# A hybrid decoder step: the sample group's RWKV state update laid out as value half x token x head, with the group norm put between the last gate chunks

## What is computed

```python
def rwkv7_step(S, inp):                    # S: value x key, 64 x 64 for each token and head
    r_t, w_t, k_t, v_t, kk_t, a_t = inp
    sa = jnp.einsum('bhvk,bhk->bhv', S, -kk_t)
    S = (S * w_t[:, :, None, :] + sa[..., None] * (kk_t * a_t)[:, :, None, :]
         + v_t[..., None] * k_t[:, :, None, :])
    return S, jnp.einsum('bhvk,bhk->bhv', S, r_t)
...
mean = jnp.mean(o, axis=-1, keepdims=True)
var = jnp.mean(jnp.square(o - mean), axis=-1, keepdims=True)
o = ((o - mean) * lax.rsqrt(var + GN_EPS)).reshape(B, T, RW_WIDTH)
o = o * gn_w + gn_b
o = (o + bonus) * g
...
m = sigmoid(g_a) * (o_a @ w_pa) + sigmoid(g_b) * (o_b @ w_pb)
x = x + gt1 * (m @ w_o)
```

## Time and profile before

| | us |
|---|---|
| median of 3 runs | 1410.02 (1409.33 to 1414.19) |
| the profiled execution: its time | 1408.94 |
| its span | 1407.2 |
| TensorE busy | 1291.8 (92%) |
| VectorE busy | 461.1 (33%) |
| ScalarE busy | 316.7 (23%) |
| GpSimd busy | 71.5 (5%) |

### The profile page before, as it was taken

The page is one execution under the profiler, slowest core; times in us unless marked ns, Lnnn a source line. Parts: engine busy times, 40 slices in busy tenths (PEclk is TensorE's granted clock), DMA queues, the critical chain, the costliest instruction groups (busy, mean ns, idle before and its releaser), DMA issues.

```text
span 1407.2 us, 21314 instructions
## 1 busy us (share of the span) xinstructions
PE 1291.8 (92%) x8359; PEld 649.1 (46%) x8359; DVE 461.1 (33%) x1061; ACT 316.7 (23%) x563; POOL 71.5 (5%) x62
## 2 busy tenths in 40 slices
PE   6999768889797999999999999999999999999997
PEld 4887457867585333333333333333333333333333
DVE  2056533333635322332233222332223322233223
ACT  3014632200102221222122211222112221122212
POOL 0000701223200000000000000000000000000000
PEclk9999988999898999999999999999999999999999
DMA  9965130047513699999999999999999999999994
GB/s 368 318 232 212 38 120 2 3 153 271 213 60 120 246 416 429 428 428 428 428 428 428 428 428 428 428 428 428 429 428 429 428 429 428 429 428 429 428 428 173
DMA packets 55362, 465.44 MB, mean 331 GB/s; under 512 B 4989, under 2 KB 7297, under 8 KB 29706
## 3 DMA queue, kind: packets, MB, share of 16 engines
q1 hardware_dynamic: 53370, 461.09, 79.0%
q0 software_dynamic: 1408, 3.63, 0.8%
q10 hardware_dynamic: 544, 0.13, 0.0%
HBM read 462.36 MB, written 3.52 MB: 331 GB/s over the span
## 4 chain that ended last, share of the span: by engine, by line
PE 49%; DMA 42%; DVE 5%; ACT 2%; issue 1%; SPq 0%; POOL 0%; DVEq 0%; ACTq 0%
DMA ring<-in_w 40%; PE ps L1207 16%; PE ps L768 7%; PE ps L1233 5%; PE ps L1161 2%; PE ps L1119 2%; DMA ring<-in_w_mod 2%; PE ps L1098 2%; PE ps L1185 2%; PE ps L1072 1%; PE ps L777 1%; PE ps L745 1%; PE ps L1215 1%; PE ps L996 1%; DMA ring<-in_w_in 1%
## 5 line engine op out<-in xcount | busy, mean ns | idle before, releaser
L1207 PE MATMUL ps<-ring,PT 128*64 128x512 f32 x2048 | 449.8, 593 | 21.8 <-DMA ring<-in_w 21.0
L1207 PEld LDWEIGHTS ps<-ring,PT 128*64 128x64 f32 x2048 | 144.8, 137 | 320.8 <-issue 271.9
L1654 DVE TENSOR_TENSOR SQ<-ps,SQ 128x528 f32<-128x528 f32 x132 | 84.2, 700 | 626.4 <-PE ps L1185 626.4
L1233 PE MATMUL ps<-ring,PT 128*64 128x512 f32 x1024 | 226.8, 595 | 0.0
L1233 PEld LDWEIGHTS ps<-ring,PT 128*64 128x64 f32 x1024 | 70.5, 137 | 133.4 <-issue 133.4
L655 ACT COPY SG<-ps 128x512 f32<-128x512 f32 x64 | 34.4, 589 | 405.6 <-PE ps L1207 405.6
L768 PE MATMUL ps<-HT,ring 128*128 128x264 f32 x448 | 107.6, 401 | 1.9 <-DMA ring<-in_w_in 1.9
L768 PEld LDWEIGHTS ps<-HT,ring 128*128 128x128 f32 x448 | 87.8, 198 | 20.1 <-issue 2.6
L1161 PE MATMUL ps<-XR,PT 128*64 128x512 f32 x396 | 94.2, 611 | 1.6 <-DVE PT L1626 1.6
L1185 PE MATMUL ps<-PT 64*128 64x264 f32 x528 | 76.3, 408 | 0.8 <-ACT PT L668 0.8
L1185 PEld LDWEIGHTS ps<-PT 64*128 64x128 f32 x528 | 45.3, 185 | 44.9 <-issue 27.6
(11 more groups left out here) (375 smaller groups left out, 1130.5 us busy)
## 6 DMA issues: line engine op xcount, KB each, us to landing
ring<-in_w SPq DMA_DIRECT2D x192, 2048.0 KB, 20.9
ring<-in_w_mod SPq DMA_DIRECT2D x12, 2048.0 KB, 14.4
ring<-in_w_in SPq DMA_DIRECT2D x9, 2048.0 KB, 8.9
ring<-in_w_o SPq DMA_DIRECT2D x2, 2048.0 KB, 16.8
ring<-in_w_pa SPq DMA_DIRECT2D x1, 2048.0 KB, 7.8
ring<-in_w_pb SPq DMA_DIRECT2D x1, 2048.0 KB, 19.7
XR<-in_x_prompt SPq DMA_DIRECT2D x2, 512.0 KB
SG<-bias_by_distance POOLq DMA_DIRECT2D x1, 1024.0 KB, 9.0
```

The costliest lines, as they stand in the source:

```text
L1207: last = mm(ps[64 * lin:64 * lin + 64, 2 + hh, :], XG[:, k % 4, k // 4, :], slot_tile(c)[:, k % 2, lin * FE + hh * 512:lin * FE + hh * 512 ...
L1233: last = mm(ps[64 * hh:64 * hh + 64, 4, :], AC[:, f, :], slot_tile(c)[:, f % 4, hh * 512:hh * 512 + 512], start=(f == 0), stop=(f == NF - 1))
L1654: v.tensor_tensor(YA[:, p::4, :], ps[:, bank:bank + 2, 0:T], YA[:, p::4, :], ALU.add).then_inc(sem["comb_used"], 1)
```

## The change

The state now lies with (value half, token, head) on the 128 partitions and 32 values x 64 keys along the free axis. A vector over keys is then one row of 64 for each partition, and VectorE reads it with a stride of zero along the values (`over_values`), a vector over values with a stride of zero along the keys (`over_keys`). The rows come about once for all six vectors: GpSimd spreads each over (token, head) columns with 24 operations of 128x8x2 (L422 of the changed kernel, into `EXP`), TensorE turns them with 12 products of 64x64 into bank 4 (L959), and ScalarE copies that into `VEC` (three copies, L590 and L592), all ahead of the scan, next to `BON`. The five rounds of `EX` and `spread` fall away. Of the update, GpSimd computes two products (`SW`, `T2`, L450 and L451), VectorE the rest, from SBUF. The output goes back to (head parity, value) partitions with one operation of 128x128 (`SOE`) and one product of 128x32 on TensorE (L1100).

The state is loaded and stored with 2 transfers in place of 8, in rows of 8 KB in place of 256 bytes. The group norm's sums move from `mixer(0)` to ahead of and between the groups of gate chunk 8, `attention_mixed` comes behind `ob_ready` as a whole, and SyncE's first expert load waits for `smp_step` 2, the new last step.

```diff
@@ gpsimd, ahead of the scan
-            for q, src in ((0, NK), (2, Aa), (3, k_mod), (4, r), (5, vv)):
-                chain(pool.tensor_copy(SMP[:, q, :, :], src[:, :, NP:T]))
+            parity = BO[:, 0::64].unsqueeze(1).broadcast_to([P, 32, 2])
+            for q, src in enumerate((NK[:, :, NP:T], dec[:, :, :], Aa[:, :, NP:T], k_mod[:, :, NP:T], r[:, :, NP:T], vv[:, :, NP:T])):
+                out = EXP[:, q, :].rearrange("p (b i s) -> p i b s", i=4, s=2)
+                for i in range(4):
+                    ins = pool.tensor_tensor(out[:, i], src[:, i, :].unsqueeze(2).broadcast_to([P, NS, 2]),
+                                             parity[:, 0:NS, :], ALU.mult)
+                chain(ins)
...
@@ gpsimd, behind the scan
-            for q in range(5):
-                pool.wait_ge(sem["o_done"], 4)
-                if q:
-                    pool.wait_ge(sem["ex_used"], q)
-                pool.tensor_tensor(
-                    EX, SMP[:, q, :, :].rearrange("p a b -> p (a b)").unsqueeze(2).broadcast_to([P, 32, CH]),
-                    II[:, 0:CH].unsqueeze(1).broadcast_to([P, 32, CH]), ALU.mult).then_inc(sem["ex_ready"], 1)
-            pool.wait_ge(sem["smp_step"], 5)
+            pool.wait_ge(sem["vec_evac"], 3)
+            pool.wait_ge(sem["o_done"], NCHUNK)
+            pool.wait_ge(sem["ld_s0"], 32)
+            pool.tensor_tensor(SW, S0, over_values(1), ALU.mult).then_inc(sem["smp_part"], 1)
+            pool.tensor_tensor(T2, over_keys(VEC[:, 5, 0:32]), over_values(3), ALU.mult).then_inc(sem["smp_part"], 1)
+            pool.wait_ge(sem["smp_step"], 1)
...
@@ scalar
+            act.wait_ge(sem["vec_done"], 1)
+            act.copy(VEC[:, 0:5, :], ps[:, 4, 0:5 * CH].rearrange("p (a b) -> p a b", b=CH)).then_inc(sem["vec_evac"], 1)
+            for vh in range(2):
+                act.copy(VEC[64 * vh:64 * vh + 64, 5, 0:32],
+                         ps[64 * vh:64 * vh + 64, 4, 5 * CH + 32 * vh:5 * CH + 32 * vh + 32]).then_inc(sem["vec_evac"], 1)
...
@@ tensor
+            for q in range(6):
+                for vh in range(2):
+                    last = mm(ps[64 * vh:64 * vh + 64, 4, q * CH:q * CH + CH], EXP[:, q, :], II[:, 0:CH], start=True, stop=True)
+            last.then_inc(sem["vec_done"], 1)
             for hp in range(4):
                 mm(ps[:, hp, 0:T], BO, TM[:, hp, :], start=True, stop=True).then_inc(sem["bon_done"], 1)
...
-            spread(0)
             project([6], range(3, 4))
             modulation(10)
-            project([7], range(0, 1))
-            spread(1)
-            project([7], range(1, 4))
-            spread(2)
+            project([7])
             modulation_transposed(10)
+            pe.wait_ge(sem["soe_ready"], 1)
+            mm(ps[:, 5, 0:32], SOE, cst[:, K_SL:K_SL + 32], start=True, stop=True).then_inc(sem["smp_o"], 1)
+            pe.wait_ge(sem["smp_step"], 2)
+            for hp in range(4):
+                mm(ps[:, 4 + hp, 0:T], BO, OT[:, hp, :], start=True, stop=True).then_inc(sem["gn_done"], 1)
             modulation(11)
-            project([8], range(0, 1))
-            spread(3)
-            project([8], range(1, 4))
-            spread(4)
+            project([8], range(0, 2))
+            pe.wait_ge(sem["gnsq_ready"], 1)
+            for hp in range(4):
+                mm(ps[:, 4 + hp, 0:T], BO, OSQ[:, hp, :], start=True, stop=True).then_inc(sem["gn_done"], 1)
+            project([8], range(2, 4))
             modulation_transposed(11)
...
@@ vector
+            dve.wait_ge(sem["ld_s0"], 32)
+            dve.wait_ge(sem["vec_evac"], 3)
+            chain(v.tensor_tensor(T1, S0, over_values(0), ALU.mult))
+            chain(v.tensor_reduce(sa, T1, AX.X, ALU.add))
+            chain(v.tensor_tensor(T1, over_keys(sa), over_values(2), ALU.mult))
+            dve.wait_ge(sem["smp_part"], 1)
+            chain(v.tensor_tensor(S0, SW, T1, ALU.add))
+            dve.wait_ge(sem["smp_part"], 2)
+            done(v.tensor_tensor(S0, S0, T2, ALU.add), "smp_step", 1)
+            chain(v.tensor_tensor(T1, S0, over_values(4), ALU.mult))
+            chain(v.tensor_reduce(so, T1, AX.X, ALU.add))
...
-            attention_mixed(range(4))
             dve.wait_ge(sem["gn_evac"], 8)
...
-            attention_mixed(range(4, KD))
+            attention_mixed(range(KD))
```

More of the change, by code:

```diff
@@ L606, in _ @@
             project([6], range(3, 4))
-            for j, m in ((7, 10), (8, 11)):
-                mod_rows(m)
-                project([j])
-                mod_columns(m)
+            mod_rows(10)
+            project([7])
+            mod_columns(10)
             for hp in range(4):
@@ L1063, in _ @@
             pe.wait_ge(sem["ot_ready"], 1)
[L1065 to L1075 removed]
             project([6], range(3, 4))
             modulation(10)
[L1078 to L1081 removed]
+            project([7])
             modulation_transposed(10)
[L1083 to L1087 removed]
+            pe.wait_ge(sem["soe_ready"], 1)
[3 more added lines that the diff above has]
+                mm(ps[:, 4 + hp, 0:T], BO, OT[:, hp, :], start=True, stop=True).then_inc(sem["gn_done"], 1)
+            modulation(11)
+            project([8], range(0, 2))
+            pe.wait_ge(sem["gnsq_ready"], 1)
+            for hp in range(4):
+                mm(ps[:, 4 + hp, 0:T], BO, OSQ[:, hp, :], start=True, stop=True).then_inc(sem["gn_done"], 1)
+            project([8], range(2, 4))
             modulation_transposed(11)
@@ L1099, in mixer @@
                     last.then_inc(sem["pab_done"], 1)
-            mixer(0, range(4))
-            pe.wait_ge(sem["smp_step"], 5)
-            for hp in range(4):
-                mm(ps[:, 4 + hp, 0:T], BO, OT[:, hp, :], start=True, stop=True).then_inc(sem["gn_done"], 1)
-            pe.wait_ge(sem["gnsq_ready"], 1)
-            for hp in range(4):
-                mm(ps[:, 4 + hp, 0:T], BO, OSQ[:, hp, :], start=True, stop=True).then_inc(sem["gn_done"], 1)
-            mixer(0, range(4, KD))
+            mixer(0, range(KD))
             pe.wait_ge(sem["ob_ready"], 1)
```

67 lines of the change are left out of this document (30 added, 37 removed).

## The result

The changed kernel took 1375.85 us in the median of four executions (1375.04 to 1377.37), the one before 1409.67 beside it (1408.56 to 1414.19): a ratio of 0.976, interval 0.974 to 0.978. What those five microseconds are is the question of this study.

A forecast was written before the change was run, and what follows sets the result against it. TensorE's work between scan and output projection was taken as the bound, the expert loop moving with it. 30.7 less 1.3 and 0.3 gives 29.1 us off the 1407.2 span; with 1.7 and 1.1 added, 1380.9, range 1376 to 1388.

The forecast's parts named there:

- The spreads: Between the scan and the mixers: four rounds at 3.43 us and one at 5.37 fall away, 19.1 us saved.
- the waits of the norm: TensorE's two waits for VectorE, ahead of the squares and of mixer(1), go away: 9.5 us saved.
- the wait below 1 us at L1100: TensorE's wait for the state's output (`soe_ready`) stays under 1 us; 0.8 was laid out for the way through.
- none at the fifth group: At mixer(0)'s fifth group TensorE's new wait for VectorE is met with 0.2 us to spare; under 1 us expected.
- the output's worst case, 319.3: If GpSimd keeps its turn for `T2`, VectorE finishes the state's output at 319.3 us; TensorE arrives at 319.1.
- The laid-out stretch, 30.7: From the scan's end to the end of `mixer(1)`, which comes at 369.5 in place of 400.17: 30.7 us saved.
- the one term that I had called undecided: Behind the scan, 2.5 us of idle time may lower TensorE's clock; a loss of 1.8 us was taken.
- more saved: Rival, 8%: clock holds behind the scan and added products cost 0.6 us: 1378 to 1379, 1377 without L1100's wait.
- The state's output: VectorE's seven operations, with GpSimd's two products beside them, start at 297.35 and end at 317.0 to 319.3 us.
- Added ahead of the scan, 1.3 + 0.3: TensorE's 12 small products cost 1.3 us (0.6 to 2.5), GpSimd's operations delaying VectorE's small ones 0.3 (0 to 2).
- The scan's end does not move in this part: In the stretch's layout VectorE's last additions of the scan still end at 297.29 us, as in the profile before.
- the neighbours: The two likeliest rivals: VectorE finishing the state's output late, 1386 to 1388 us (11%), and more saved (8%).

The follow-up runs named there:

- `norm_back`: The changed kernel with the group norm back inside mixer(0) and attention_mixed split again: 1389.18 us, 0.9865 of the kernel before.
- both repeats: The changed kernel, unchanged, profiled again in two later runs: 1380.93 us and 1379.89 us.
- `dummy_spread3`: The changed kernel with 12 unread products of 128x512, three spreads' worth, behind groups of gate chunk 7: 1386.61 us, 0.9858 of the kernel before.
- `dve_all`: The changed kernel with GpSimd's two products, SW and T2, computed by VectorE instead: 1375.26 us, 0.9771 of the kernel before.
- `after_hold`: The changed kernel with six unread products in TensorE's 3.05 us of idle time ahead of the scan: 1375.25 us, 0.9769 of the kernel before.
- the two filled kernels: The changed kernel and the one before, each with six unread products in TensorE's idle time ahead of the scan: 1375.25 and 1408.8 us.
- `best_a`: The changed kernel with chunk 7's weights loaded once their slot is free, and chunk 6's last quarter and modulation 10 ahead of two waits: 1375.53 us, 0.9761.

## Why the prediction was right, and where it failed

*The mechanism.* Right, but for the clock behind the scan. The spreads (3.43 each given back and paid in full), the waits of the norm (12 us with it put back), the loop that moves with TensorE, the wait below 1 us at L1100 (0.35), no wait for the squares and none at the fifth group all came. The prediction put the output's worst case, 319.3, "at TensorE's arrival, 319.1, or under it"; it is 0.2 above, which changed nothing, since the output came earlier than either case. A start of `project` at a clock below 1 did not come in the first profile.

*The laid-out stretch, 30.7.* It was 32.2 in the first profile and 354.25 + 14.40 - 295.34 = 73.3, so 30.9, in the second. The difference is the one term that I had called undecided, 1.8 for a fallen clock less the 0.3 to 0.5 that the weights' landing takes of it. At that very idle time of 2.53 us the clock fell in three of the seven profiles with this code (`norm_back` and both repeats, not the first profile, `dummy_spread3`, `dve_all` and `after_hold`). There was no right answer to choose: the term is 0 or 1.3, by execution. The rival "more saved" had it at 0 and came at 1378 to 1379, or 1377 with no wait at L1100; it had 8%, too little for one side of an even choice, and even it lies above 1375.85, because of the term below that no rival held.

*The state's output.* 317.0 to 319.3 was forecast for a start at 297.35, so 19.7 to 22.0 behind it; it took 315.26 - 296.14 = 19.1. The first product took 3.86 where 4.15 was laid out, and `T2` ended 7.35 behind VectorE's start where 7.75 was (`SW` took 4.51 for 4.7).

*Added ahead of the scan, 1.3 + 0.3.* Mis-sized. From the first row of this stage (223.41; 223.55) to the second L992 (233.90; 234.91) the changed kernel takes 0.87 more, 0.87 again between the two filled kernels, and 0.87 in the kernel before with the 12 products alone. So the whole cost is TensorE's. GpSimd's 24 operations take 0.19 each and end at 165.5, and VectorE's small operations beside them, from 162 to 166 us, took as long as before.

*The step that failed.* "The scan's end does not move in this part", with the sum made against one profile as though the same code had one length. The profile of before held the long low clock at 240 us (1.7 us); the first profile after held the short one, at no cost. From the inverses' last row to the scan's end it was 24.50 before and 24.01 after, 0.5, of which 0.3 is a gap in issue (0.92; 0.60); the changed kernel's two other profiles have 24.02 and 24.83 there, the second with a gap of 1.17. With 0.7 for the mis-sized products and a start 0.1 later that is 1.7 + 0.5 + 0.7 - 0.1 = 2.8, the whole miss ahead of the scan's end. The changed kernel's own profiles differ by about as much in the first two (1.55 and 0.8), so no change of code is needed for them; only the 0.7 is a cost of the change. One rival stays open: its 12 products may shift the odds at 240 us. With them the short form came in six of ten unfilled profiles, and without them there is one such profile, with the long form. The second failed term is the clock's 1.8 behind the scan, taken at the costlier side: it measured 0, which is 1.3 to 1.5 of the miss. The last 0.85 is between span and median.

*The size of the miss.* Over all eleven executions the changed kernel's median is 1377.4 (1372.4 to 1382.3), that of the kernel before 1409.1 over 41 (1404.0 to 1415.9). Against these the forecast of 1381 is 3.6 us too high and its range holds. That it holds is in part luck: the range was made of the neighbours and the added work, and had no term for what executions of one code differ by, which is 10 us here. Four executions in a row that lay within 2.4 us of each other were no measure of that spread.

*What stays open.* Why the low clock takes the short or the long form wasn't shown. The Trainium skill, TensorE: Matmul & The Clock Gate, Part 1, says that the gate's timing runs freely and isn't started by the kernel, so that the point of change depends on where the work falls; the traces agree as far as like code had unlike clocks. Executions also start the same stage up to 4.0 us apart (the small products at 219.54 in `best_a`, 223.55 in the first profile). The start alone doesn't decide the form: the products behind the 3.05 us began at 235.93, 237.28, 237.31, 237.50, 238.73 and 239.94 where the short form came, and at 238.21, 238.88, 238.93, 238.95 and 239.35 where the long one did.

## What to carry to other kernels

A state update whose vectors lie along the free axis with stride zero needs no large matrix product for each of its steps; here 12 small ones, once, cost 0.9 us and five spreads of 3.4 us fell away. What it costs is VectorE's time, which is free as long as TensorE has that much other work (1.4 us were to spare here), so put the output's user behind that work. Move a normalisation's sums up between independent groups of products: here that was worth 12 to 13 us and added no work. And before a sum is made against a profile, mark in it each idle time of TensorE from 2.5 us on, each run of shorter waits (3.39 and 1.63 in a row, or 0.96 and 0.76, stood ahead of slow products here), and the slow products behind them: here those terms were drawn anew in each execution. An idle time that a change removes or fills takes its draw with it, as the rows at 240 us show. Whether the executions then lie closer together isn't shown: five of the filled kernel lie within 3.4 us, and the changed kernel's first four lay within 2.4.

## What the hardware showed that I had not expected

- With 2.53 us of idle time ahead of like products, the granted clock stayed at 1.00 in four profiles and fell in three (3.80 and 5.49 us for the same eight products). Behind 4.38 it fell in the one profile that has it, and behind the 3.38 of the kernel before in three of three (5.37, 5.37 and 6.39 us for a spread that takes 3.43).
- The first group of expert products took 13.95 to 13.96 us in eleven profiles and 15.53 to 15.58 in three, behind only 0.76 us of idle time in each; the profiles differ in how long the clock was low.
- Behind 3.05 us of idle time the clock was low in all eleven profiles that kept it, but for two forms of it, one free of cost and one of 1.55 to 1.7 us. Filled with unread products, it stayed at 1.00 in three of three.
- GpSimd's product of 128x2048 with one stride-zero operand took 4.51, beside VectorE's work on operands in PSUM up to 296.1 and its wait from then on. Its second one, 5.67, consists of 2.2 us of waiting for VectorE and 3.5 of work.
- In the changed kernel's three profiles and in `best_a` the waiting engine came next each time: VectorE behind `SW`, GpSimd behind VectorE's product, VectorE behind `T2`. VectorE's reduction, which reads one operand, took its 2.29 us beside the running `T2`.
